# A second mixer's output projection with tokens on partitions, and its norm by token tile

## The chip, the cores and the metric

The kernel runs on one core of one Trainium2 chip. The core has TensorE (PE in the profile), VectorE (DVE), ScalarE (ACT), GpSimd (POOL) and SyncE (SP), a memory of 128 partitions (SBUF) and eight accumulator banks (PSUM), each 512 float32 columns wide, called `pb[0]` to `pb[7]` here. The metric is the device time of the whole program in microseconds, lower is better.

## What is computed

Two blocks in a row on 512 tokens of width 1024, all in float32. The first is an attention block with a feed-forward part, the second is this, and the change lies at its middle:

```python
def second_block(x, ...):
    hn = rms_norm(x, norm_mix_pre)
    mix = hybrid_mixer(hn, ...)               # y = [y_a, y_b]; returns y @ w_out
    x = x + rms_norm(mix, norm_mix_post)
    hn = rms_norm(x, norm_ffn_pre)
    ff = conv_ffn(hn, w_gate, w_up, conv_w, conv_b, w_down)
    return x + rms_norm(ff, norm_ffn_post)

def rms_norm(x, g):
    return x * lax.rsqrt(jnp.mean(x * x, axis=-1, keepdims=True) + EPS) * g

# in hybrid_mixer: four mLSTM heads and four gated linear attention heads of width 128
y_a = sigmoid(a_o) * head_rms_norm(h_fw + h_bw, mlstm_norm)
y_b = silu(b_r) * head_rms_norm(o_fw + o_bw, gla_norm)
y = concatenate([y_a, y_b])                   # 512 tokens x 1024
return y @ w_out
```

`conv_ffn` multiplies hn with two matrices of 1024x2816, runs a convolution over three tokens on one product, and feeds the gated product to `w_down`.

## The kernel before

**Numbers.** Every float32 matmul is three: each operand is split into a high part (rounded for PE's fast float format) and a low part, and `mm3` (L464) adds high*high, low*high and high*low. `AH`/`AL` are the parts of the feed-forward's input, `YH`/`YL` those of the mixer's output, `WH`/`WL` those of the weights.

**Weights.** All weights come as units of 128x1024 float32 (512 KB). There are six slots (`NS`). SP loads unit u into slot u modulo 6 of `RAW` as soon as unit u-6 has been used (`s_used`). GpSimd splits each: a copy into `WH` (L419), a subtraction into `WL` (L422); PE waits for it in `ready`. GpSimd's order is written out by hand, with a few waits by which it is held back; here it gates four heads (L450), makes four low parts of the linear attention heads (L454), waits until all four mLSTM heads are gated (`s_ym`), and splits the rest without further holds.

**Layout.** The residual `X` has features on partitions: 8 tiles (`DK`) of 128 features x 512 tokens. A norm needs a sum over partitions, which PE makes. For the usual norms the sum is wanted late: ACT squares the tiles (L1208), DVE adds them up into `ACC` (L1759, L1762), PE multiplies `ACC` with a constant matrix (`statistic`, L527), ACT takes the root and DVE the reciprocal (`RS`, L1779), which scales the products after the matmul.

**The place of the change.** It begins when the last mLSTM head is done. DVE finishes the heads: the sum of the two directions (L2323), the squares per head (L2242, L2243), the opening by the output gate (L2333), the reciprocal of all sixteen columns (L2390), the gating of each (L2267). PE turns each head (`turn_output`, L1115), ACT makes its high part (L1644) and DVE its low part (L2349). Under this PE starts the output projection with the four linear attention heads: four units side by side in `pb[0]` to `pb[3]`, feature tile m of the result against all 512 tokens; the other four follow one by one. ACT takes each finished bank twice, squared (L1208) and scaled into `MIX` (L1721), and DVE adds up the squares. Then comes the norm "post": PE sums with one-column matmuls (`root_columns`, L542), ACT and DVE make four diagonal matrices of the reciprocal roots, PE broadcasts them (`root_broadcast`, L553), and for each of the eight tiles DVE scales `MIX` (L2403) and adds it to `X` (L2404). ACT makes `AH` (L1206), DVE `AL` (L1752) and the next norm's sum of squares.

**The feed-forward behind it** has 22 chunks (`FC`) of two units (gate and up), which use the banks in three pairs. Its first two chunks, four units, run side by side (L499 to L502), feature tile by feature tile as `AH` and `AL` become ready, with the norm's `statistic` in front of the last tile. In the first block's feed-forward the first two chunks run one after the other, and the statistic stands between the two units of the second.

Of the kernel before, what the change touches and what calls it, by code (L numbers as in the profile page):

```python
# [97 lines left out]
WB = 4  # L98
# [6 lines left out]
def build(nc, dram, out):  # L105

    ctx = ExitStack()
    with ctx:
# [105 lines left out]
        MIX = put("MIX", [P, DK, T], F32, S_at + 32 * KB)  # L214
# [75 lines left out]
        ALL = ("mix", "ffn", "ple", "mix2", "post", "ffn2")  # L290
        SPLIT = tuple(n for n in ALL if n != "post")

        LAST = ("post",)

        def stages(w, names, per, fewer=()):

            s, counts = sem(f"s_{w}"), [per - (n in fewer) for n in names]
            return {n: Stage(s, sum(counts[:i])) for i, n in enumerate(names)}

        s_x = stages("x", ("ffn", "ple", "mix2", "ffn2"), DK)  # L300
        s_gh, s_gl = stages("gh", SPLIT, DK), stages("gl", SPLIT, DK)
# [38 lines left out]
        def state(h, m):  # L340
# [22 lines left out]
        s_vb, s_aof, s_dd, s_ee, s_lv, s_gs, s_gb, s_sad, s_sao, s_go, s_oc, s_ybq = (  # L363
            sem(f"s_{w}") for w in ("vb", "aof", "dd", "ee", "lv", "gs", "gb", "sad", "sao", "go", "oc", "ybq"))
        s_apad, s_a1, s_a3, s_aqk, s_br, s_va, s_zero = (
            sem(f"s_{w}") for w in ("apad", "a1", "a3", "aqk", "br", "va", "zero"))
        s_bc, s_ms2, s_ad, s_w, s_sw, s_mo, s_hb, s_hf, s_hst, s_gn, s_y2t, s_y2h, s_y2l = (
# [43 lines left out]
        def _(pool):  # L411
# [51 lines left out]
        def _(pe):  # L463
# [70 lines left out]

            def root_columns(n):

                ge(pe, s_acc[n], DK - 1)
                for part, src in enumerate((ACC, SQ[:, 1, :])):
                    if part:
                        ge(pe, s_sq[n], DK)  # L540
                    for t in range(NT):
                        ins = nc.tensor.matmul(pb[6][:, t:t + 1], src[:, tokens(t)], INVD[:, 0:1],  # L542
                                               start=(part == 0 and t == 0), stop=(part == 1 and t == NT - 1),
                                               skip_group_check=True)
                ins.then_inc(s_ms[n].sem, 1)

            def root_broadcast(n):
                for t in range(NT):
                    if t < 2:
                        ge(pe, s_diag[n], t + 1)  # L550
                    else:
                        ge(pe, s_adiag[n], t - 1)
                    ins = nc.tensor.matmul(RSP[:, tokens(t)], INVD, DIAG[:, t, :], start=True, stop=True)  # L553
                ins.then_inc(s_bcast[n].sem, 1)
# [303 lines left out]
            for m in range(DK):  # L858
# [9 lines left out]
                if m == 3:  # L868
                    statistic("ple")
# [1701 lines left out]
```

## Time and profile before

| | us |
|---|---|
| median of 3 runs | 1296.03 |
| lowest and highest | 1295.74, 1297.51 |
| the profiled execution | 1295.97 |
| its span | 1294.1 |
| PE busy | 1275.6 (99%) |
| DVE busy | 683.8 (53%) |
| GpSimd busy | 756.2 (58%) |
| ACT busy | 394.2 (30%) |

All times below are microseconds from the start of the profiled execution's span. A row of the chain or of a timeline gives the start, then the length. PE's matmuls are pipelined: the next starts before the last has left the array, so the pace is read from start to start, not from the length. PEclk is the granted clock of TensorE, 1.00 for 2.4 GHz and 0.50 for 1.2 GHz. An instruction that waits is not shown as busy; what released it stands in brackets.

### The profile page before, as it was taken

How to read it: one execution, taken by the hardware profiler on the slowest of the kernel's cores; microseconds unless marked ns; L12 is line 12 of the kernel's file. 1: busy time of each engine (PE TensorE's matmuls, PEld its weight loads, DVE VectorE, ACT ScalarE, POOL GpSimd, SP SyncE). 2: the span in 40 equal slices, each digit the busy share in tenths (PEclk: the TensorE clock that was granted, in tenths of full speed). 3: DMA queues.
4: the chain of work that ended last, by engine and by line, in shares of the span. 5: the costliest groups of instructions: out<-in, count | busy, mean ns of one | idle time of the engine just before them, and what ended most of it. 6: DMA issues, size and time to landing. Idle time of an engine off the chain costs nothing.

```text
span 1294.1 us, 16113 instructions
## 1 busy us (share of the span) xinstructions
PE 1275.6 (99%) x6432; PEld 1042.4 (81%) x6432; DVE 683.8 (53%) x923; ACT 394.2 (30%) x716; POOL 756.2 (58%) x448
## 2 busy tenths in 40 slices
PE   8999999999999999999999999999899999999998
PEld 6888877788888888888888888778788888888886
DVE  5453563887444432123467878684678644447003
ACT  4332474322111111003346365573332211110002
POOL 6855533676666646668665445224649766666660
PEclk9999999999999999999999999999899999999999
DMA  7222211323233323334333122102133223323331
GB/s 287 82 70 78 82 50 50 114 83 97 98 98 98 98 79 107 93 97 132 96 100 99 50 82 82 34 18 82 49 130 94 95 94 96 98 95 98 98 98 65
DMA packets 34207, 117.85 MB, mean 91 GB/s; under 512 B 3812, under 2 KB 4324, under 8 KB 34004
## 3 DMA queue, kind: packets, MB, share of 16 engines
q1 hardware_dynamic: 32976, 114.66, 28.1%
q10 hardware_dynamic: 1156, 2.16, 0.5%
q8 instruction: 51, 0.84, 0.3%
q14 instruction: 24, 0.20, 0.1%
HBM read 114.71 MB, written 2.10 MB: 90 GB/s over the span
## 4 chain that ended last, share of the span: by engine, by line
PE 95%; DVE 3%; ACT 1%; DMA 1%; issue 1%; POOL 0%; SPq 0%; DVEq 0%; ACTq 0%
PE PS L465 28%; PE PS L467 28%; PE PS L466 28%; PE PS L1082 1%; PE PS L967 1%; DVE ACC L1762 1%; PE PS L691 1%; PE PS L668 1%; PE PS L499 1%; PE PS L558 1%; PE PS L500 1%; PE PS L502 1%; PE PS L679 1%; PE PS L950 1%; DMA RAW<-in_w 1%
## 5 line engine op out<-in xcount | busy, mean ns | idle before, releaser
L422 POOL TENSOR_TENSOR WL<-RAW,WH 128x1024 fp32r<-128x1024 f32 (+1 forms) x216 | 509.3, 2358 | 18.0
L419 POOL TENSOR_SCALAR WH<-RAW 128x1024 fp32r<-128x1024 f32 (+1 forms) x216 | 234.4, 1085 | 446.5 <-DMA RAW<-in_w 402.3
L465 PE MATMUL PS<-AH,WH 128*128 128x512 f32 x896 | 351.2, 392 | 2.3 <-POOL WL L422 1.3
L467 PE MATMUL PS<-AH,WL 128*128 128x512 f32 x896 | 348.9, 389 | 0.0
L466 PE MATMUL PS<-AL,WH 128*128 128x512 f32 x896 | 348.7, 389 | 0.0
L465 PEld LDWEIGHTS PS<-AH,WH 128*128 128x128 f32 x896 | 168.2, 188 | 40.6 <-POOL WL L422 2.1
L467 PEld LDWEIGHTS PS<-AH,WL 128*128 128x128 f32 x896 | 168.2, 188 | 35.2
L466 PEld LDWEIGHTS PS<-AL,WH 128*128 128x128 f32 x896 | 168.2, 188 | 34.7 <-issue 0.2
L1407 ACT ACTIVATE TMP<-PAD,PRM 128x512 f32<-128x512 f32 x44 | 35.9, 817 | 125.9 <-DVE PAD L2015 125.9
L1412 ACT ACTIVATE SH<-TMP 128x512 fp32r<-128x512 f32 x44 | 27.8, 632 | 136.9 <-DVE TMP L2030 136.9
L465 PE MATMUL PS<-SH,WH 128*128 128x512 f32 x176 | 68.5, 389 | 0.0
L466 PE MATMUL PS<-SL,WH 128*128 128x512 f32 x176 | 68.5, 389 | 0.0
L467 PE MATMUL PS<-SH,WL 128*128 128x512 f32 x176 | 68.5, 389 | 0.0
L465 PE MATMUL PS<-WH,SH 128*128 128x512 f32 x176 | 68.5, 389 | 0.0
L466 PE MATMUL PS<-WL,SH 128*128 128x512 f32 x176 | 68.5, 389 | 0.0
L467 PE MATMUL PS<-WH,SL 128*128 128x512 f32 x176 | 68.5, 389 | 0.0
L2030 DVE TENSOR_TENSOR TMP<-TMP 128x512 f32<-128x512 f32 x44 | 62.7, 1426 | 7.3 <-ACT TMP L1410 2.8
L2010 DVE TENSOR_TENSOR TMP<-PS,RS 128x512 f32<-128x512 f32 x44 | 30.2, 687 | 67.9 <-PE PS L467 67.9
L2021 DVE SCALAR_TENSOR_TENSOR TMP<-PAD,PRM,TMP 128x512 f32<-128x512 f32 x44 | 44.7, 1015 | 36.6 <-ACT TMP L1407 36.6
L2015 DVE TENSOR_TENSOR PAD<-PS,RS 128x512 f32<-128x512 f32 x44 | 30.3, 688 | 53.1 <-PE PS L467 53.0
L1410 ACT ACTIVATE TMP<-TMP 128x512 f32<-128x512 f32 x44 | 27.8, 633 | 90.3 <-DVE TMP L2024 90.3
L1762 DVE TENSOR_TENSOR ACC<-ACC,SQ 128x512 f32<-128x512 f32 x41 | 47.2, 1150 | 14.0 <-ACT SQ L1208 12.4
(365 smaller groups left out, 2033.0 us busy)
## 6 DMA issues: line engine op xcount, KB each, us to landing
RAW<-in_w SPq DMA_DIRECT2D x185, 512.0 KB, 3.5
RAW<-in_w SPq DMA_DIRECT2D x16, 384.0 KB, 3.0
RAW<-in_w SPq DMA_DIRECT2D x16, 320.0 KB, 2.9
X<-in_x SPq DMA_DIRECT2D x4, 512.0 KB, 6.9
BT<-in_bias SPq DMA_DIRECT2D x1, 2048.0 KB, 9.4
out<-FX SPq DMA_DIRECT2D x4, 256.0 KB, 2.1
out<-FX ACTq DMA_DIRECT2D x4, 256.0 KB, 2.0
PIN<-in_p ACTq DMA_DIRECT2D x1, 512.0 KB, 3.4
```

The source lines that it names most:

```text
L419: nc.gpsimd.tensor_scalar(WH[:, slot, 0:width], RAW[:, slot, 0:width], 1.0, 1.0, ALU.mult, ALU.mult).then_inc(s_hi, 1)
L422: nc.gpsimd.tensor_tensor(WL[:, slot, 0:width], RAW[:, slot, 0:width], WH[:, slot, 0:width].bitcast(F32), ALU.subtract).then_inc(s_split, 1)
L465: nc.tensor.matmul(o, lh, rh, start=start, stop=False)
L466: nc.tensor.matmul(o, lh, rl, start=False, stop=False)
L467: return nc.tensor.matmul(o, ll, rh, start=False, stop=stop)
L1407: A(TMP[:, j, :], PAD[:, j, 0:T], ACT.Identity, bias=prm_at("fcb" + sfx, 0, i, 2, j), scale=prm_at("fcw" + sfx, 0, i, 2, j)).then_inc(S["t ...
L1410: A(TMP[:, j, :], TMP[:, j, :], func).then_inc(S["act"].sem, 1)
L1762: V_.tensor_tensor(ACC[:], ACC[:], SQ[:, j % 2, :], ALU.add).then_inc(s_acc[n].sem, 1)
L2010: V_.tensor_tensor(TMP[:, 2 + j, :], pb[2 * ((2 * i + j) % FB) + 1], RS[:], ALU.mult).then_inc(S["up"].sem, 1)
L2015: V_.tensor_tensor(PAD[:, j, o:o + T], pb[2 * ((2 * i + j) % FB)], RS[:], ALU.mult).then_inc(S["pad"].sem, 1)
L2021: V_.scalar_tensor_tensor(t, PAD[:, j, 1:T + 1], prm_at("fcw" + sfx, FC, i, 2, j), t, ALU.mult, ALU.add).then_inc(S["ta"].sem, 1)
L2030: V_.tensor_tensor(TMP[:, 2 + j, :], TMP[:, j, :], TMP[:, 2 + j, :], ALU.mult).then_inc(S["h"].sem, 1)
```

## The change

It has seven parts.

1. The output projection has tokens on partitions. A unit of weights is now 128 rows of `w_out` in the order `MIXED`, one for each head, and a bank holds 128 tokens x 512 features: banks 2t and 2t+1 are token tile t. `mixed_block` adds one head's product to one bank. PE does six heads for tiles 0 and 1 first, while the heads are turned, then the rest, so that the tiles end one after the other.
2. The norm "post" is made by token tile. ACT squares both banks of a tile with a running sum, takes the root, DVE the reciprocal, ACT writes the scaled product to `MIX`, PE turns it back with eight transposes into the same two banks (`turn_mixed`), and DVE adds it to `X` with the gain (`mixed_added`). The column sums, diagonal matrices and the broadcast are gone.
3. `AH` and `AL` are made in two token sets, tokens 0 to 255 and 256 to 511, eight tiles each.
4. The first chunk of the second feed-forward runs first for one set, then for the other (matmuls of 256 columns); the second chunk runs as a chunk of its own, with the statistic between its two units. The squares for it are made and added after the last `AL`.
5. GpSimd no longer waits for the gated mLSTM heads; it now waits for the last `AL` before it splits the feed-forward's unit 4.
6. The first mLSTM head's root, reciprocal and gating come ahead of the others' squares; the opening and gating of the others are interleaved.
7. The statistic of the first feed-forward stands one unit later, the one of the norm behind it two products later.

The diff, cut to its core:

```diff
-            pool.wait_ge(s_ym, H2)
-            split_range(UNITS["wo2"][0] + 4, UNITS["ffn2"][0] + NS)
-
-            split_range(UNITS["ffn2"][0] + NS, NU)
+            split_range(UNITS["wo2"][0] + 4, UNITS["ffn2"][0] + 4)
+            ge(pool, s_gl["ffn2"], 2 * DK)
+            split_range(UNITS["ffn2"][0] + 4, NU)
...
-                        if root is not None and w == 0:
+                        if root is not None and w == (norm == "ffn"):
                             statistic(root)
...
-                    pe.wait_ge(s_mix, DK)
-                    side_by_side(u0, range(4), AH, AL, (s_gh[norm], s_gl[norm]), {DK - 1: lambda: statistic(norm)})
+                    for u in (u0, u0 + 1):
+                        ready(u)
+                    for part, c in enumerate((FIRST, REST)):
+                        for k in range(DK):
+                            if part == 0 and k == 6:
+                                turn_mixed(NT - 1)
+                            ge(pe, s_gl[norm], DK * part + k + 1)
+                            for w in range(2):
+                                s = (u0 + w) % NS
+                                ins = mm3(pb[w][:, c], WH[:, s, tokens(k)], WL[:, s, tokens(k)], AH[:, k, c],
+                                          AL[:, k, c], k == 0, k == DK - 1)
+                                if part and k == DK - 1:
+                                    ins.then_inc(s_used, 1)
+                    chunk(1, None, norm)
...
-                if m == 3:
+                if m == 5:
                     statistic("ple")
...
                     pe.wait_ge(s_ym, n - H2 + 1)
+                    pe.wait_ge(s_hf, H2)
...
+            def mixed_block(n, t, half, stop=False):
+                k, s, c = MIXED[n], (uw + n) % NS, slice(half * T, (half + 1) * T)
+                return mm3(pb[2 * t + half], YH[:, k, tokens(t)], YL[:, k, tokens(t)], WH[:, s, c], WL[:, s, c],
+                           n == 0, stop)
+
+            def turn_mixed(t):
+                pe.wait_ge(s_pmx, t + 1)
+                for half in range(2):
+                    for q in range(4):
+                        ins = nc.tensor.transpose(pb[2 * t + half][:, tokens(q)], MIX[:, t, tokens(4 * half + q)], IDENT)
+                    ins.then_inc(s_ptt, 1)
+
+            for n in range(6):
+                if n >= 3:
+                    turn_output(H2 + n - 3)
+                ready(uw + n)
+                if n < H2:
+                    pe.wait_ge(s_y2p, n + 1)
                 else:
-                    pe.wait_ge(s_y2l, k + 1)
+                    pe.wait_ge(s_y2l, n - H2 + 1)
+                for t in range(2):
+                    for half in range(2):
+                        mixed_block(n, t, half)
+            turn_output(2 * H2 - 1)
...
+            mixed_pair(6, 2)
+            turn_mixed(0)
+            mixed_pair(7, 2).then_inc(s_mix, 1)
+            turn_mixed(1)
+            mixed_pair(4, 3).then_inc(s_used, 1)
+            mixed_pair(5, 3).then_inc(s_used, 1)
+            turn_mixed(2)
+            mixed_pair(6, 3).then_inc(s_used, 1)
+            mixed_pair(7, 3).then_inc(s_used, 1)
...
+            def mixed_root(t):
+                if t < NT - 1:
+                    act.wait_ge(s_mix, t + 1)
+                else:
+                    act.wait_ge(s_used, UNITS["wo2"][0] + DK)
+                link(A(SQ[:], PS[:, 2 * t:2 * t + 2, :], ACT.Square, accum_out=PSS[:, t:t + 1]))
+                A(PRT[:, t:t + 1], PSS[:, t:t + 1], ACT.Sqrt, bias=EPS_C, scale=1.0 / D).then_inc(s_prt, 1)
...
             for m in range(DK):
-                act.wait_ge(s_used, UNITS["wo2"][0] + m + 1)
-                norm_tile("post", None, m // 2, 2, m % 2, None, x=pb[m % WB], split=False)
-                A(MIX[:, m, :], pb[m % WB], ACT.Copy, scale=prm("post2", m)).then_inc(s_mix, 1)
-            root_of_columns("post")
-            x_tiles("ffn2", "fpre2", AH)
+                if m >= 2:
+                    ge(act, s_acc["ffn2"], m - 1)
+                A(SQ[:, m % 2, :], X[:, m, :], ACT.Square).then_inc(s_sq["ffn2"].sem, 1)
...
+            inverse_roots(0)
+            gated(0)
+            state_squares(1)
             state_sum(H2 - 1)
             state_squares(H2 - 1)
...
+            state_squares(H2 - 2)
+            state_opened(1)
+            inverse_roots(1)
+            gated(1)
+            state_opened(H2 - 2)
+            gated(2)
+            low_turned(range(0, 1))
+            state_opened(H2 - 1)
+            gated(3)
+            low_turned(range(1, H2))
...
+            for k in range(DK):
+                token_low(0, k)
+            mixed_added(2, 0)
+            mixed_reciprocal(3)
+            mixed_added(2, 1)
+            mixed_added(3, 0)
+            mixed_added(3, 1)
+            for k in range(DK):
+                token_low(1, k)
             for m in range(DK):
...
+                add_square("ffn2", m // 2, 2, m % 2)
```

The order on the engines shows it best at three places. The first is GpSimd's queue from the low parts of the linear attention heads on (`YL<-BR,YH`), before:

```order
L454 TENSOR_TENSOR YL<-BR,YH 128x512 [waits s_y2h] x3
L419 TENSOR_SCALAR WH<-RAW 128x1024 [waits s_raw3,s_used,s_ym]
L422 TENSOR_TENSOR WL<-RAW,WH 128x1024 [waits s_hi]
L419 TENSOR_SCALAR WH<-RAW 128x1024 [waits s_raw4,s_used]
L422 TENSOR_TENSOR WL<-RAW,WH 128x1024 [waits s_hi]
```

and with the change:

```order
L452 TENSOR_TENSOR YL<-BR,YH 128x512 [waits s_y2h] x3
L417 TENSOR_SCALAR WH<-RAW 128x1024 [waits s_raw3,s_used]
L420 TENSOR_TENSOR WL<-RAW,WH 128x1024 [waits s_hi]
L417 TENSOR_SCALAR WH<-RAW 128x1024 [waits s_raw4,s_used]
L420 TENSOR_TENSOR WL<-RAW,WH 128x1024 [waits s_hi]
...
L417 TENSOR_SCALAR WH<-RAW 128x1024 [waits s_raw4,s_used]
L420 TENSOR_TENSOR WL<-RAW,WH 128x1024 [waits s_hi]
L417 TENSOR_SCALAR WH<-RAW 128x1024 [waits s_raw5,s_used,s_gl]
L420 TENSOR_TENSOR WL<-RAW,WH 128x1024 [waits s_hi]
```

The wait `s_ym` (the gated heads) has gone from the split behind the `YL` row, and a wait `s_gl` (all `AL`) stands at the split of the ninth unit behind it, unit 4 of the feed-forward.

The second is DVE behind the projection: what scales and adds the product (`MIX`, `X`), makes `AL` and adds the squares (`ACC<-ACC,SQ`). Before, a tile of 512 tokens at a time:

```order
L2403 TENSOR_TENSOR MIX<-MIX,PS 128x512 [waits s_mix,s_bcast]
L2404 TENSOR_TENSOR X<-X,MIX 128x512 [waits s_vc]
L2403 TENSOR_TENSOR MIX<-MIX,PS 128x512 [waits s_mix]
L2404 TENSOR_TENSOR X<-X,MIX 128x512 [waits s_vc]
L1752 SCALAR_TENSOR_TENSOR AL<-X,PRM,AH 128x512 [waits s_gh]
L1759 COPY ACC<-SQ 128x512 [waits s_sq]
L2403 TENSOR_TENSOR MIX<-MIX,PS 128x512 [waits s_mix]
L2404 TENSOR_TENSOR X<-X,MIX 128x512 [waits s_vc]
L1752 SCALAR_TENSOR_TENSOR AL<-X,PRM,AH 128x512 [waits s_gh]
L1762 TENSOR_TENSOR ACC<-ACC,SQ 128x512 [waits s_acc,s_sq]
```

With the change, adds of 128x128 (`X<-PS,PRM,X`), then the two sets:

```order
L2455 SCALAR_TENSOR_TENSOR X<-PS,PRM,X 128x128 [waits s_ptt] x4
L2462 SCALAR_TENSOR_TENSOR AL<-X,PRM,AH 128x256 [waits s_gh] x8
L2455 SCALAR_TENSOR_TENSOR X<-PS,PRM,X 128x128 [waits s_ptt] x4
L2448 RECIPROCAL COL<-COL 128x1 [waits s_prt]
L2455 SCALAR_TENSOR_TENSOR X<-PS,PRM,X 128x128 [waits s_ptt] x12
L2462 SCALAR_TENSOR_TENSOR AL<-X,PRM,AH 128x256 [waits s_gh] x8
L1802 COPY ACC<-SQ 128x512 [waits s_sq]
L1805 TENSOR_TENSOR ACC<-ACC,SQ 128x512 [waits s_acc,s_sq] x7
L1814 RECIPROCAL RS<-RS 128x512 [waits s_sd]
```

The adds into `ACC`, which stood between the `AL`, now stand behind the sixteenth.

The third is PE around the statistic of the second feed-forward (`PS<-ACC,CST`). Before, in front of the last tile of the four units that run side by side:

```order
L502 MATMUL PS<-AL,WH 128x512 [waits s_gl]
L502 MATMUL PS<-AL,WH 128x512 x3
L527 MATMUL PS<-ACC,CST 128x512 [waits s_acc]
L499 MATMUL PS<-AH,WH 128x512 [waits s_gh]
L500 MATMUL PS<-AH,WL 128x512
...
L502 MATMUL PS<-AL,WH 128x512 [waits s_gl]
L502 MATMUL PS<-AL,WH 128x512 x3
L465 MATMUL PS<-AH,WH 128x512 [waits s_split]
```

With the change, from the last tile of the second set on; the cut leaves out the rest of one unit's 24 matmuls:

```order
L462 MATMUL PS<-AH,WH 128x256 [waits s_gl]
L463 MATMUL PS<-AL,WH 128x256
L464 MATMUL PS<-AH,WL 128x256
...
L462 MATMUL PS<-AH,WH 128x512 [waits s_split]
L463 MATMUL PS<-AL,WH 128x512
L464 MATMUL PS<-AH,WL 128x512
...
L464 MATMUL PS<-AH,WL 128x512
L524 MATMUL PS<-ACC,CST 128x512 [waits s_acc]
L462 MATMUL PS<-AH,WH 128x512 [waits s_split]
```

It stands 24 matmuls behind the last one that waits for an `AL`.

## Rows read from the trace of the kernel before

**Rows 1.** The page, part 1 and one group of part 5: busy us, mean ns, idle before
```profile
PE 1275.6 (99%) x6432; PEld 1042.4 (81%) x6432; DVE 683.8 (53%) x923; ACT 394.2 (30%) x716; POOL 756.2 (58%) x448
...
L465 PEld LDWEIGHTS PS<-AH,WH 128*128 128x128 f32 x896 | 168.2, 188 | 40.6 <-POOL WL L422 2.1
```

**Rows 2.** Windows: stretch, its length, busy us (instructions) by engine, PEclk, DMA share, GB/s
```profile
921.00:921.60 0.60, 0.60 (x4) 0.60 (x5) 0.11 (x1) 0.00 (x0) 0.60 (x1) 0.77 0.00 0
...
925.80:931.70 5.90, 5.90 (x14) 4.64 (x15) 5.87 (x8) 2.84 (x5) 1.29 (x1) 0.51 0.01 3
```

**Rows 3.** The chain that ended last: start us, us, what
```profile
889.93 0.44 PE PS L1115 x4
...
917.60 1.75 PE PS L542 x16
...
920.98 1.80 PE PS L553 x8
...
925.77 0.77 PE PS L499
...
936.00 0.91 PE PS L502 x4
...
947.79 0.86 PE PS L527 x2
```

**Rows 4.** Timeline of PE: start us, us, line, operation, [idle before, releaser]
```profile
871.23 0.48 PE L465 MATMUL PS<-YH,WH 128*128 128x512 f32 x1
...
880.09 0.66 PE L1115 MATMUL PS<-CST,YM 128*128 128x128 f32 x4 [0.42 <-DVE YM L2267]
...
195.22 0.28 PE L668 MATMUL PS<-KL,QH 64*128 64x256 f32 x2
195.33 0.28 PE L668 MATMUL PS<-KH,QL 64*128 64x256 f32 x2
```

**Rows 5.** Timeline of DVE, end of the mixer and the norm behind it
```profile
873.98 0.20 DVE L2317 RECIPROCAL COL<-COL 128x8 f32<-128x8 f32 x1
...
875.97 1.12 DVE L2323 SCALAR_TENSOR_TENSOR YM<-PS,COL,TMP 128x128 f32<-128x128 f32 x4
...
879.34 1.29 DVE L2267 SCALAR_TENSOR_TENSOR YM<-YM,COL 128x512 f32<-128x512 f32 x2
...
924.79 0.67 DVE L2403 TENSOR_TENSOR MIX<-MIX,PS 128x512 f32<-128x512 f32 x1
925.50 2.14 DVE L2404 TENSOR_TENSOR X<-X,MIX 128x512 f32<-128x512 f32 x1
927.57 0.74 DVE L1752 SCALAR_TENSOR_TENSOR AL<-X,PRM,AH 128x512 fp32r<-128x512 f32 x1
...
930.54 0.68 DVE L1762 TENSOR_TENSOR ACC<-ACC,SQ 128x512 f32<-128x512 f32 x1
```

**Rows 6.** Timeline of GpSimd, the same stretch
```profile
867.64 5.11 POOL L454 TENSOR_TENSOR YL<-BR,YH 128x512 fp32r<-128x512 f32 x4 [15.49 <-DVE WT L2281]
886.16 1.04 POOL L419 TENSOR_SCALAR WH<-RAW 128x1024 fp32r<-128x1024 f32 x1 [13.41 <-DVE YM L2267]
...
897.47 1.05 POOL L419 TENSOR_SCALAR WH<-RAW 128x1024 fp32r<-128x1024 f32 x1 [4.28 <-DMA RAW<-in_w]
...
924.41 2.68 POOL L422 TENSOR_TENSOR WL<-RAW,WH 128x1024 fp32r<-128x1024 f32 x1
```

**Rows 7.** Timeline of ACT: square and scaled copy of one 512-column bank
```profile
893.83 0.60 ACT L1208 ACTIVATE SQ<-PS 128x512 f32<-128x512 f32 x1 [2.73 <-PE PS L467]
894.32 0.68 ACT L1721 ACTIVATE MIX<-PS,PRM 128x512 f32<-128x512 f32 x1
```

**Rows 8.** Timelines of DVE, GpSimd and PE in the first feed-forward block
```profile
241.93 14.12 DVE L1762 TENSOR_TENSOR ACC<-ACC,SQ 128x512 f32<-128x512 f32 x7
...
241.57 1.16 POOL L419 TENSOR_SCALAR WH<-RAW 128x1024 fp32r<-128x1024 f32 x1 [7.02 <-DVE AL L1752]
...
256.10 1.13 PE L527 MATMUL PS<-ACC,CST 128*128 128x512 f32 x2 [0.57 <-DVE ACC L1762]
```

More of the change, by code:

```diff
@@ L213, in build @@
         WT = put("WT", [P, 3, 2, T], F32, R + 32 * KB)
[L214 removed]
+        MIX = put("MIX", [P, NT, D], F32, S_at + 32 * KB)
         FX = put("FX", [P, NT, D], F32, A_at)
@@ L532, in statistic @@
                 ins.then_inc(s_ms[n].sem, 1)
[L535 to L554, printed above, removed]
             def column_sums(o, src, weights, width):
@@ new lines, in _, with mixed_pair @@
+            turn_output(2 * H2 - 1)
+            def mixed_pair(n, t):
+                for half in range(2):
+                    ins = mixed_block(n, t, half, n == DK - 1)
+                return ins
+            pe.wait_ge(s_y2l, 2)
+            mixed_pair(0, 2)
+            mixed_pair(1, 2)
+            pe.wait_ge(s_y2l, H2)
+            mixed_pair(0, 3).then_inc(s_used, 1)
+            mixed_pair(1, 3).then_inc(s_used, 1)
+            for n in (2, 3):
+                mixed_pair(n, 2)
+                mixed_pair(n, 3).then_inc(s_used, 1)
@@ new lines, in _ @@
+            for n in (4, 5):
+                mixed_pair(n, 2)
+            for n in (6, 7):
+                ready(uw + n)
+                for t in range(2):
+                    ins = mixed_pair(n, t)
+                    if n == 7:
+                        ins.then_inc(s_mix, 1)
+            mixed_pair(6, 2)
[4 more added lines that the diff above has]
+            mixed_pair(5, 3).then_inc(s_used, 1)
@@ L1386, in _ @@
                 mixed_high(j)
-            def x_tiles(n, gain, hi):
-                for m in range(DK):
-                    norm_tile(n, gain, m // 2, 2, m % 2, hi)
             for m in range(DK):
@@ L1664, in scaled_states, with mixed_roots @@
                 ins.then_inc(s_hst, 1)
+            def mixed_roots(part):
+                act.wait_ge(s_mq, part + 1)
+                m = MSS[:, ROOTS[part]]
+                A(m, m, ACT.Sqrt, bias=EPS_C, scale=1.0 / DV).then_inc(s_gn, 1)
             stabilisers_copied(0)
@@ L2389, in _ @@
-            dve.wait_ge(s_gn, 2)
-            link(V_.reciprocal(MSS, MSS))
-            gated(0)
-            for h in range(H2):
-                if h + 1 < H2:
-                    gated(h + 1)
-                low_turned(range(h, h + 1))
-            for m in range(DK - 1):
-                add_square("post", m // 2, 2, m % 2)
-            column_reciprocal("post")
-            ge(dve, s_bcast["post"], 1)
-            for m in range(DK):
-                dve.wait_ge(s_mix, m + 1)
-                link(V_.tensor_tensor(MIX[:, m, :], MIX[:, m, :], RSP, ALU.mult))
-                V_.tensor_tensor(X[:, m, :], X[:, m, :], MIX[:, m, :], ALU.add).then_inc(s_x["ffn2"].sem, 1)
-                if m:
-                    low("ffn2", "fpre2", (m - 1) // 2, 2, (m - 1) % 2, AH, AL)
-                    add_square("ffn2", (m - 1) // 2, 2, (m - 1) % 2)
@@ new lines, in mixed_added, with token_low @@
+            def mixed_added(t, half):
+                for q in range(4):
+                    k = 4 * half + q
+                    dve.wait_ge(s_ptt, 2 * t + half + 1)
+                    x = X[:, k, tokens(t)]
+                    ins = V_.scalar_tensor_tensor(x, pb[2 * t + half][:, tokens(q)], prm("post2", k), x, ALU.mult, ALU.add)
+                    if t % 2:
+                        ins.then_inc(s_x["ffn2"].sem, 1)
+            def token_low(part, k):
+                c = REST if part else FIRST
+                ge(dve, s_gh["ffn2"], DK * part + k + 1)
+                V_.scalar_tensor_tensor(AL[:, k, c], X[:, k, c], prm("fpre2", k), AH[:, k, c].bitcast(F32),
+                                        ALU.mult, ALU.subtract).then_inc(s_gl["ffn2"].sem, 1)
@@ new lines, in _ @@
+            mixed_reciprocal(0)
+            for t in range(2):
+                mixed_added(t, 0)
+                mixed_reciprocal(t + 1)
+                mixed_added(t, 1)
+            for k in range(DK):
+                token_low(0, k)
[4 more added lines that the diff above has]
+            mixed_added(3, 1)
+            for k in range(DK):
+                token_low(1, k)
+            for m in range(DK):
+                add_square("ffn2", m // 2, 2, m % 2)
```

106 lines of the change are left out of this document (47 added, 59 removed).

## The prediction

> **What bounds the kernel now.** The first view is the page: PE is busy for 99% of the span [rows 1], so time is lost only where PE stops, does extra work, or runs on a slower clock. The second is the chain that ended last, read from the second mixer's output projection to the first two chunks of the second feed-forward block. It runs through matmuls except at one place [rows 3]. PE starts the projection at 871.23 [rows 4]; the last column sums of its norm start at 917.60 and take 1.75; a wait of 1.6 follows, the broadcast takes 1.80 from 920.98, and the next matmul starts at 925.77, 3.0 later. The third is the windows view: the granted clock is at 0.77 in 921.0 to 921.6, so it fell from 2.4 to 1.2 GHz there, after sixteen one-column matmuls and the wait of 1.6, and it is still at 0.51 in 925.8 to 931.7 [rows 2]. 5.7 us of resumed matmuls at half speed lose 2.85. The statistic of the next norm ends at 948.65, and twelve more matmuls of 0.2275 (four take 0.91 [rows 3]) end the two chunks at 951.4. That is my milestone; behind it PE has nothing to wait for up to the end of the span, with or without the change.
>
> Over the pure work the stretch holds: a wait of 0.5 at the first turned head [rows 4], 1.75, 1.6, 1.8, 3.0 and 2.85, together **11.5 us**. That is the most this change can win here.
>
> **What the matmuls cost after it.** The projection keeps 192 matmuls of 512 columns. Of the first two chunks, one keeps 48, the other becomes 96 of 256 columns. No row shows a full-height 256-column one. The nearest is a pair of 64-row ones, 0.11 apart [rows 4], which would be half of 0.2275; the other end is the mean duration of a weight load, 0.188 [rows 1]. I take 0.115, since weight loads of the four turned tiles follow each other at 0.11 (0.44 for four [rows 3]), though each lasts longer: +0.1 for 96. The upper end costs 96 times 0.073, 7.0. The Trainium skill (TensorE: Matmul & The Clock Gate, LDWEIGHTS) puts a weight load of 128 columns at 107 ns; no row here shows that duration, and an estimate from that page would make the sum 0.6 less.
>
> **The norm's new form.** 32 transposes at 0.11 are **+3.5**. They replace 1.75 and 1.8 of PE work and the waits of 1.6 and 3.0. A token tile's chain is a square of 1024 columns, a root, a reciprocal and a scaled copy. From 0.60 and 0.68 for 512 columns [rows 7] I take 1.03 and 1.2 (bounds: no growth, and double), with 0.45 for the two small steps: 2.7. Behind the first tile PE has 12 matmuls, 2.73, so it waits 0.15 to 0.25. At the second tile the reciprocal stands on DVE behind four adds (1.12 for four from PSUM [rows 5]), and PE has only the first turn and 6 matmuls: 0.75. The third tile has 12 matmuls over it: nothing. Together **+1.0**. These adds have one input in PSUM, and such an operation kept 0.67 while GpSimd worked [rows 5, 6].
>
> **The second token set.** PE ends the first set and turns the fourth tile inside it. DVE must then do eight adds (2.25) before the first AL of the rest. PE comes there at 871.23 + 43.7 (192 matmuls) + 1.76 (turned heads) + 3.65 (waits at them, below) + 1.0 + 2.64 (24 transposes) = 924.0 for the first set, whose 48 matmuls and 8 transposes last 5.5 + 0.9: 930.4. The fourth tile is turned after 36 of these, from 928.1 to 929.0; DVE's adds behind the halves end at 930.9 and the first AL at 931.3: **+0.95**. From there PE needs 48 times 0.115, 5.5, while DVE makes the other seven AL in some 2.5 (half of 0.74 [rows 5] and a start each). So the last AL is done 2.5 after the first, and PE arrives behind the first unit of the next chunk at 5.5 plus 24 times 0.2275, **8.45 us after the last AL**.
>
> **The statistic.** PE needs all eight squares added up there, and DVE adds none before the last AL. Before, these adds lay between the AL, and GpSimd had nothing to split from 927.1 on, since its slots were full. Now the last AL is just what GpSimd waits for. The first feed-forward block already has this arrangement: GpSimd starts its splits at 241.57, with the last AL, and seven adds take 14.12, to 256.05 [rows 8]; one alone takes 0.68 [rows 5]. So the adds end 14.5 after the last AL and **PE waits 14.5 - 8.45 = 6.1**. Even in the first block, where more matmuls lie over them, PE waited 0.57 [rows 8]. The queue behind the waiting statistic holds the next 24 matmuls, and nothing can overtake it. The raw halves of units 4 and 5 are long in their slots then (a load lands some 3.6 after its slot is free [rows 6]), so GpSimd does have work. A wait of 6.1 is longer than the 3.7 from the last wide matmul to 921.3, when the clock fell [rows 2, 3]; I take the same loss as before, **+2.85** (bounds 0 and 2.85).
>
> **The heads.** GpSimd's wait for the gated heads goes. Its YL end at 872.75 and its next split stood until 886.16 [rows 6]; now two splits fill 872.8 to about 880.9. DVE's chain there has two inputs in SBUF at each square, gating and opening. The price of the overlap is read off one such operation: X<-X,MIX took 2.14, where an add alone takes 0.68 [rows 5], while GpSimd's subtraction ran from 924.41 [rows 5, 6]; it ended only behind it. Laid out so, with reciprocal done at 874.1 [rows 5]: the first head is gated at 877.2 instead of 875, sum of the fourth head (which the turn now also waits for) at 880.4, second gating at 884.8, first YL at 886.75. PE arrives at 879.4, 883.6 and 885.3, so it waits 1.0, 1.25 and 1.4: **+3.65**. With no overlap it would wait only 0.9, at the first YL, as that now stands behind two gatings. The Trainium skill (SBUF — State Buffer, Who interferes with whom) says that a DVE operation with both inputs in SBUF takes an exclusive lock against GpSimd's reads, for whole instructions. No row shows this for the gating itself; by that rule the head waits stand at 3.65 and not at 0.9.
>
> **Splits.** Units 6 and 7 of the projection are loaded when the third and fourth token tiles release units 0 and 1, at 897.4 and 898.8, are split by 904.5 and 908.0, and PE needs them at 906.75 and 909.5: cover 1.5 at the least.
>
> **Elsewhere.** The first block's statistic one unit later takes away its 0.57: **-0.6**. The third statistic, two products later, had no wait and has none; what it feeds is needed far later, I take 0 (bounds 0 and 1).
>
> **The sum.** After: 3.5 + 1.0 + 0.95 + 6.1 + 2.85 + 3.65 + 0.1 = 18.15. Less 11.5 and 0.6: **+6.05**. The profiled execution took 1295.97, within 0.1 of the median 1296.03, so 1302.0.
>
> **Rivals.** (1) Faster: the adds do not meet the splits as they did in the first block. The point is 1.15 us an add: below it, seven adds and a copy are done within 8.45 and PE never waits. Alone they cost 0.68, 4.8 in all. Then 6.1 and 2.85 go: 1293.1, and 1290.3 if the heads escape the overlap too. Against it stands that forms, sizes and the starting event are those of the first block. (2) The wait comes, the clock holds: 1299.2. For it: PE did no narrow matmuls ahead. (3) 256-column matmuls cost a weight load each: 7.0 more, of which the slower second set takes 3.5 off the statistic's wait: 1305.5. Against it, the transposes' 0.11. (4) Overlaps are half of what I take, and gain and loss cancel: 1296.
>
> **Chances.** Forecast 0.50 (own range 1299.5 to 1304.5), (1) 0.20, (2) 0.13, (3) 0.10, (4) 0.07. The range 1292.5 to 1305.5 leaves out the better half of (1) and the tail of (3). A measurement of this kernel tells some 0.2%, 2.6 us, from no change. Faster 0.20, within it 0.16 (case 4, part of 2, the edge of the forecast), slower 0.64.
>
> **What would show it.** Right: PE idle some 6 us before the second block's statistic, released by ACC; seven adds in some 14 us beside splits; a granted clock near 0.5 right behind; three waits of over a microsecond at the turned heads. Each is wrong alone if its row reads otherwise. The whole is wrong if the adds run at under 1.15 each; the chain would then go through matmuls from 872 on, and all that is left of the 11.5 are transposes and waits of 9.2.

## The result and the profile after

The changed kernel takes **1302.95 us** (median of 6 runs, 1300.27 to 1304.77) where the kernel before takes 1296.77 (6 runs, 1295.29 to 1298.17): a ratio of 1.0052, interval 1.0041 to 1.0064. It is slower, by 6.2 or 0.5%. Its profiled execution took 1300.27, the fastest of the six, with a span of 1298.4.

The timeline of PE at the turned heads, the turned token tiles, the second token set and the statistic (columns as in [rows 4]; before, the first of these places had one wait of 0.42, and [rows 3] shows the others):

```profile
878.42 0.63 PE L1104 MATMUL PS<-CST,YM 128*128 128x128 f32 x4 [0.74 <-issue]
...
882.90 0.66 PE L1104 MATMUL PS<-CST,YM 128*128 128x128 f32 x4 [1.10 <-DVE YM L2302]
...
884.99 0.47 PE L462 MATMUL PS<-WH,YH 128*128 128x512 f32 x1 [1.43 <-DVE YL L2386]
...
912.22 1.09 PE L1137 MATMUL PS<-CST,MIX 128*128 128x128 f32 x8 [0.16 <-ACT MIX L1746]
...
930.16 0.39 PE L462 MATMUL PS<-AH,WH 128*128 128x256 f32 x1 [0.78 <-DVE AL L2462]
...
941.25 0.39 PE L464 MATMUL PS<-AH,WL 128*128 128x512 f32 x1
947.41 2.07 PE L524 MATMUL PS<-ACC,CST 128*128 128x512 f32 x2 [5.77 <-DVE ACC L1805]
948.50 1.42 PE L462 MATMUL PS<-AH,WH 128*128 128x512 f32 x1
```

The first stop stands as "issue", that is, its row names no releaser. By the code the turn also waits for the fourth head's sum (`s_hf`), and DVE's row of it ends at 878.32, 0.10 ahead of PE:

```profile
877.20 1.12 DVE L2358 SCALAR_TENSOR_TENSOR YM<-PS,COL,TMP 128x128 f32<-128x128 f32 x4
```

The long wait is the predicted one, and its releaser is the add into `ACC`. DVE and GpSimd in the same stretch show why (the answering rows of before are [rows 5, 6], and the pattern is that of [rows 8]):

```profile
932.80 0.42 DVE L1802 COPY ACC<-SQ 128x512 f32<-128x512 f32 x1
933.32 14.04 DVE L1805 TENSOR_TENSOR ACC<-ACC,SQ 128x512 f32<-128x512 f32 x7
```

```profile
932.97 1.17 POOL L417 TENSOR_SCALAR WH<-RAW 128x1024 fp32r<-128x1024 f32 x1 [4.36 <-DVE AL L2462]
934.22 2.71 POOL L420 TENSOR_TENSOR WL<-RAW,WH 128x1024 fp32r<-128x1024 f32 x1
936.90 1.49 POOL L417 TENSOR_SCALAR WH<-RAW 128x1024 fp32r<-128x1024 f32 x1
```

GpSimd's splits start with the last `AL`, and the chain of waits shows the adds in step with them: they last about 1.36 and 2.71 in turn, and each of the seven ends 0.54 to 0.56 behind the end of a GpSimd instruction (934.68 behind 934.14, 937.48 behind 936.93).

```profile
933.32 1.36 DVE ACC L1805
934.77 2.71 DVE ACC L1805
937.58 1.35 DVE ACC L1805
939.03 2.71 DVE ACC L1805
```

The windows view (columns as in [rows 2]) shows the clock: the fall of before at 921 is gone, and it is at 0.50 around the resumed matmuls instead.

```profile
921.00:921.60 0.60, 0.60 (x4) 0.50 (x3) 0.60 (x3) 0.56 (x2) 0.27 (x1) 1.00 0.57 157
943.50:944.50 1.00, 0.00 (x0) 0.00 (x0) 1.00 (x1) 0.33 (x1) 1.00 (x1) 0.86 0.84 344
944.50:950.00 5.50, 2.59 (x4) 1.46 (x5) 2.75 (x2) 0.47 (x1) 5.42 (x4) 0.50 0.04 11
...
950.60:951.20 0.60, 0.60 (x3) 0.50 (x2) 0.60 (x1) 0.00 (x0) 0.54 (x1) 0.63 0.00 0
951.20:956.00 4.80, 4.80 (x22) 3.95 (x22) 4.44 (x4) 1.62 (x2) 1.86 (x1) 1.00 0.00 0
```

The ledger against the trace. The stretch from the projection's first matmul to the end of the first two chunks was 80.02 (871.23 to 951.25) and is 86.30 (869.26 to 955.56). Each term is read from start to start here, since the idle time in brackets counts from the modelled end of the last matmul and leaves out 0.16 to 0.26 of each stop (941.25 + 0.23 to 947.41 is 5.93, the bracket says 5.77).

| term, us | predicted | measured |
|---|---|---|
| 32 transposes | 3.5 | 3.5 (eight take 0.79, and the next wide matmul 0.09 more) |
| waits at the turned token tiles | 1.0 | 1.1 |
| second token set | 0.95 | 0.95 |
| the second statistic | 6.1 | 5.95 |
| half clock behind it | 2.85 | 1.8 |
| turned heads | 3.65 | 3.85 (0.90, 1.26, 1.69) |
| 96 matmuls of 256 columns | 0.1 | 0.6 (0.12 apart) |
| what was there before | -11.5 | -11.5 (taken over, not read anew) |
| sum | +6.65 | +6.25, the stretch grew by 6.28 |
| ahead of the projection | -0.6 | -1.97 |
| profiled execution, milestone | +6.05 | +4.31 |

### The profile page after: what moved, and what is told of

Its sections match the earlier page's. It is cut to its first block, busy times and chain, and to the rows that moved or that the text cites. A ratio compares the mean times of both kernels' runs of the same rounds, so it can differ in the third digit from the quotient of the medians.

```text
span 1298.4 us, 16239 instructions
## 1 busy us (share of the span) xinstructions
PE 1275.3 (98%) x6488; PEld 1043.1 (80%) x6488; DVE 677.9 (52%) x942; ACT 395.0 (30%) x722; POOL 751.6 (58%) x448
## 4 chain that ended last, share of the span: by engine, by line
PE 94%; DVE 3%; ACT 1%; DMA 1%; issue 0%; POOL 0%; SPq 0%; DVEq 0%; ACTq 0%
PE PS L462 29%; PE PS L464 28%; PE PS L463 28%; PE PS L1070 1%; PE PS L955 1%; DVE ACC L1805 1%; PE PS L667 1%; PE PS L644 1%; PE PS L534 1%; PE PS L655 1%; PE PS L938 1%; DMA RAW<-in_w 1%; PE PS L1051 0%; PE PS L929 0%; PE PS L540 0%
## 5 line engine op out<-in xcount | busy, mean ns | idle before, releaser
L417 POOL TENSOR_SCALAR WH<-RAW 128x1024 fp32r<-128x1024 f32 (+1 forms) x216 | 231.3, 1071 | 455.7 <-DMA RAW<-in_w 420.9
L462 PE MATMUL PS<-AH,WH 128*128 128x512 f32 (+1 forms) x944 | 367.9, 390 | 3.5 <-DVE AL L1795 1.5
L464 PE MATMUL PS<-AH,WL 128*128 128x512 f32 (+1 forms) x944 | 364.3, 386 | 0.0
L463 PE MATMUL PS<-AL,WH 128*128 128x512 f32 (+1 forms) x944 | 364.3, 386 | 0.0
L462 PEld LDWEIGHTS PS<-AH,WH 128*128 128x128 f32 x944 | 177.6, 188 | 43.3 <-issue 3.0
L464 PEld LDWEIGHTS PS<-AH,WL 128*128 128x128 f32 x944 | 177.5, 188 | 36.2
L463 PEld LDWEIGHTS PS<-AL,WH 128*128 128x128 f32 x944 | 177.6, 188 | 35.8 <-issue 0.8
L2065 DVE TENSOR_TENSOR TMP<-TMP 128x512 f32<-128x512 f32 x44 | 55.0, 1251 | 7.0 <-ACT TMP L1423 2.8
L2068 DVE TENSOR_TENSOR SL<-TMP,SH 128x512 fp32r<-128x512 f32 x44 | 36.5, 829 | 30.7 <-ACT SH L1425 30.7
```

The lines of the kernel that those rows point to most:

```text
L417: nc.gpsimd.tensor_scalar(WH[:, slot, 0:width], RAW[:, slot, 0:width], 1.0, 1.0, ALU.mult, ALU.mult).then_inc(s_hi, 1)
L462: nc.tensor.matmul(o, lh, rh, start=start, stop=False)
L463: nc.tensor.matmul(o, lh, rl, start=False, stop=False)
L464: return nc.tensor.matmul(o, ll, rh, start=False, stop=stop)
L2065: V_.tensor_tensor(TMP[:, 2 + j, :], TMP[:, j, :], TMP[:, 2 + j, :], ALU.mult).then_inc(S["h"].sem, 1)
L2068: V_.tensor_tensor(at(SL, i, j, 2), TMP[:, 2 + j, :], at(SH, i, j, 2).bitcast(F32), ALU.subtract).then_inc(S["sl"].sem, 1)
```

## The experiments

Kernels of before beside the three groups of runs took 1296.21 (21 runs), 1295.83 (28) and 1295.87 (26). Each experiment starts from the changed kernel unless it says otherwise.

**1. GpSimd held until the adds are done.**

```
-            ge(pool, s_gl["ffn2"], 2 * DK)
+            ge(pool, s_acc["ffn2"], DK)
```

> The changed kernel, but GpSimd stays held until DVE has added the last square of the second feed-forward's norm, and not only until the last AL. Theory (the seven adds meet GpSimd's splits): the adds take some 4.8 us instead of 14.0, PE does not wait at the statistic, the granted clock stays at 1.00; the wait of 5.8 and 1.75 of half clock go, 1303.0 becomes about 1295.5, ratio to the kernel before 0.999. Rival (the adds are slow by themselves, or ACT's squares set their pace): they stay at 14, the statistic waits as before, 1303. Second rival (GpSimd starts 5 us later and PE waits for unit 4 instead): the wait moves to the start of the third chunk, and less than half is won.

Measured: 1294.94 (11 runs), ratio 0.9993 (0.9984 to 1.0002). DVE's timeline:

```profile
933.76 5.47 DVE L1805 TENSOR_TENSOR ACC<-ACC,SQ 128x512 f32<-128x512 f32 x7
```

PE does not wait at the statistic. The mean clock of the profiled execution is 1.0, that of the ten others 0.996 to 0.998. One line of waiting moved on GpSimd is worth 8.0 in the medians (7.6 by the ratios); the 5.95 and the 1.8 of clock behind it make 7.75. The splits start 6.4 later (939.32 for 932.97) and cost nothing: PE waits for none.

**2. The statistic 24 matmuls later.**

```
-                        if root is not None and w == (norm == "ffn"):
+                        if root is not None and w == 1:
```

> The changed kernel, but the second feed-forward's statistic stands one unit (24 matmuls, 5.45 us) later; the splits still run beside the adds. Theory (only the place of the statistic against the end of the adds matters): the adds still take 14.0, PE waits 0.3 to 0.6 at the statistic, the clock stays at 1.00, about 1296.0, ratio 0.999. Rival (the slow adds or the late reciprocal root cost PE elsewhere, at the banks): less than 4 us is won.

Measured: 1295.99 (11 runs), ratio 0.9994 (0.9985 to 1.0002). The adds are as slow as ever, and PE is there only 0.4 too early (timelines of DVE and of PE):

```profile
935.64 14.11 DVE L1805 TENSOR_TENSOR ACC<-ACC,SQ 128x512 f32<-128x512 f32 x7
```

```profile
949.80 1.13 PE L524 MATMUL PS<-ACC,CST 128*128 128x512 f32 x2 [0.40 <-DVE ACC L1805]
```

So the cost sits in where PE asks for the sum, not in DVE's time. This is the other cure for the same collision.

**3. Work in place of the wait.** If the clock falls because PE stands idle, it should hold when PE works through that time. The 24 extra matmuls go to the free bank `pb[7]`, and nothing reads them.

```
+                            if norm == "ffn2":
+                                ready(u + 1)
+                                for k in range(DK):
+                                    mm3(pb[7], WH[:, (u + 1) % NS, tokens(k)], WL[:, (u + 1) % NS, tokens(k)],
+                                        AH[:, k, :], AL[:, k, :], k == 0, k == DK - 1)
```

> The changed kernel with 24 more matmuls of 512 columns into an unused bank in front of the second feed-forward's statistic; their result is not used. They last 5.45 us and lie in the wait of 5.8. Theory (the idle time costs twice: the wait, and the half clock behind it): the wait shrinks to some 0.3, the adds end when they did, the clock stays at 1.00, and 1.75 us are won for added work: 1301.2, ratio 1.0035. Rival (the clock's loss is not due to the idle time): no gain, 1303.

Measured: 1301.64 (5 runs), ratio 1.0041 (1.0029 to 1.0054). A window that holds the end of the adds, in this kernel:

```profile
943.50:950.00 6.50, 6.10 (x25) 4.40 (x24) 4.35 (x4) 1.32 (x2) 6.42 (x3) 1.00 0.18 71
```

The clock stays at 1.00. From the statistic to the sixth matmul behind it PE now takes 2.12 (947.95 to 950.07), in the changed kernel 3.84 (947.41 to 951.25): 1.7 less, the clock's own share, which agrees with the 1.8 of the ledger and is below my 2.85. The median falls by 1.3, but the intervals of the two ratios overlap, so the time alone does not show it; the traces do.

**4. Why the adds are slow: their squares in PSUM.** GpSimd's hold is that of the change; only ACT writes the squares to two free banks.

```
-                A(SQ[:, m % 2, :], X[:, m, :], ACT.Square).then_inc(s_sq["ffn2"].sem, 1)
+                A(pb[6 + m % 2], X[:, m, :], ACT.Square).then_inc(s_sq["ffn2"].sem, 1)
...
+                sq = pb[6 + j % 2] if n == "ffn2" else SQ[:, j % 2, :]
...
-                    V_.tensor_tensor(ACC[:], ACC[:], SQ[:, j % 2, :], ALU.add).then_inc(s_acc[n].sem, 1)
+                    V_.tensor_tensor(ACC[:], ACC[:], sq, ALU.add).then_inc(s_acc[n].sem, 1)
```

> The changed kernel, with only the place of the second norm's squares changed: ACT writes them into the two banks pb[6] and pb[7], which are free then, instead of SBUF, and DVE adds them up from there. GpSimd is held back no longer than in the changed kernel, so its splits still run beside all seven adds. Theory: an add is stretched by a split because both its inputs lie in SBUF; with one in PSUM it takes its 0.7, the seven take 5 us beside splits, and the statistic's wait and the half clock go: 1294.9, as with GpSimd held (1294.94). Rival: the splits stretch whatever DVE does there, by the traffic as such; then the adds stay at 14 and the time at 1302.5. In between (adds of 1.15 to 1.5) the wait would be 0 to 3.

Measured: 1294.91 (11 runs), ratio 0.9992 (0.9984 to 1.0001). DVE and GpSimd side by side:

```profile
937.00 5.44 DVE L1806 TENSOR_TENSOR ACC<-ACC,PS 128x512 f32<-128x512 f32 x7
```

```profile
936.39 1.05 POOL L417 TENSOR_SCALAR WH<-RAW 128x1024 fp32r<-128x1024 f32 x1 [4.37 <-DVE AL L2463]
937.52 2.41 POOL L420 TENSOR_TENSOR WL<-RAW,WH 128x1024 fp32r<-128x1024 f32 x1
939.91 1.04 POOL L417 TENSOR_SCALAR WH<-RAW 128x1024 fp32r<-128x1024 f32 x1
```

The same seven adds beside the same splits take 5.44 instead of 14.04, and the splits take 1.05 and 2.41 instead of 1.49 and 2.71. The operation, its size and its neighbour are unchanged; what changed is the place of the second input, and with it where ACT writes. ACT's writes are not the cause: in experiment 1 they go to SBUF as before and the adds take 5.47. So for these adds the condition is that both inputs lie in SBUF while GpSimd splits. The Trainium skill (SBUF — State Buffer, Who interferes with whom) says that a DVE instruction with two SBUF inputs contends with a GpSimd instruction that reads SBUF, and one with at most one such input does not. The traces agree, with 14.04 against 5.44.

**5. The first head's low part first.** DVE makes it right behind the second gating, ahead of the other openings.

```
             gated(1)
+            low_turned(range(0, 1))
             state_opened(H2 - 2)
             gated(2)
-            low_turned(range(0, 1))
```

> The changed kernel, but DVE makes the first mLSTM head's low part right behind the second head's gating and not behind the third's. Theory (the low part stands behind an opening and a gating that nobody waits for): PE's wait of 1.4 at the fifth head's product falls to some 0.2 and nothing else moves, -1.2 us, 1301.8, ratio 1.004. Rival (the next turned head or the fourth gating becomes late): less than 0.5 won, with a new wait at a later turned head.

Measured: 1301.33 (5 runs), ratio 1.0041 (1.0028 to 1.0053). The wait of 1.43 is gone, but the one at the second turned head is 2.14 in this execution:

```profile
884.56 0.89 PE L1104 MATMUL PS<-CST,YM 128*128 128x128 f32 x4 [2.14 <-DVE YM L2302]
```

On its own it is not told from no effect (the ratios' intervals overlap). Together with experiment 1 it is:

> The changed kernel with two edits that were also run alone: GpSimd held until the squares of the second norm are added up (alone: 1294.9), and the first head's low part ahead of the openings of the others (alone: 1301.3 against 1302 to 1303). The second one only moved a wait in its own run (2.14 at the second turned head in the place of 1.10 and 1.43). If the head waits are worth nothing to order within DVE's chain, the time is that of the first edit: 1294.9; if each microsecond of the low part's wait counts, it is 1293.8.

Measured: **1292.81** (10 runs), ratio 0.9972 (0.9963 to 0.9981), below experiment 1 by more than the intervals, and below both of my numbers. I had taken its wait as merely moved. From start to start the head stops are 0.87, 1.28 and 1.68 in experiment 1, 3.8 together, and one of 2.30 here: 1.5 less. Experiment 4's execution, in which DVE's rows at the heads last as long as here, has stops of 2.30 and 1.68: 1.7 less. The medians differ by 1.6 (changed kernel) and 2.1 (experiment 1). This is the lowest median of all kernels here, 3 below the kernel before; two that follow (1293.0 and 1293.16) are not told from it.

**6. No splits beside the heads.** GpSimd splits the projection's units 4 and 5 ahead of its work for the linear attention heads.

```
-            split_range(UNITS["ffn"][0] + 3, UNITS["wo2"][0] + 4)
+            split_range(UNITS["ffn"][0] + 3, UNITS["wo2"][0] + 5)
...
+            split_range(UNITS["wo2"][0] + 5, UNITS["wo2"][0] + 6)
...
-            split_range(UNITS["wo2"][0] + 4, UNITS["ffn2"][0] + 4)
+            split_range(UNITS["wo2"][0] + 6, UNITS["ffn2"][0] + 4)
```

> The changed kernel, but GpSimd splits the projection's units 4 and 5 ahead of its work for the linear attention heads (one before the products into YB, one before the YL), so that it has no split left beside DVE's chain of the mLSTM heads. Theory, from the profile of the changed kernel: the gating there takes 2.77 and 1.52 where it would take 1.4 and 1.3 alone, because each ends only with a split; the three head waits (0.74, 1.10 and 1.43, together 3.27) shrink to 1.0 or less, and the time is 2.3 below the changed kernel's: 1300.5 with 1296.2 for the kernel before. Rival: the chain of operations, not the overlap, sets these waits; then they stay within 0.5 of 3.27 and the time stays at 1302.5. The statistic's wait grows by nothing in either case: 5.8 stays.

Measured: 1302.45 (6 runs), ratio 1.0054 (1.0035 to 1.0074). The time is the rival's, the mechanism is not. PE has no wait at the heads, and DVE's gating and square take 0.69 and 0.68:

```profile
878.05 0.69 DVE L2303 SCALAR_TENSOR_TENSOR YM<-YM,COL 128x512 f32<-128x512 f32 x1
878.66 0.68 DVE L2278 TENSOR_TENSOR TMP<-YM 128x512 f32<-128x512 f32 x1
```

In the changed kernel these two stood beside splits:

```profile
872.34 2.77 DVE L2302 SCALAR_TENSOR_TENSOR YM<-YM,COL 128x512 f32<-128x512 f32 x1
875.03 1.52 DVE L2277 TENSOR_TENSOR TMP<-YM 128x512 f32<-128x512 f32 x1
```

But both splits now fall beside DVE's work inside the mLSTM loop. Unit 5's raw half lands only at 858.3; beside its split four operations take 3.90 that took 1.14, and PE waits:

```profile
858.58 3.90 DVE L2359 SCALAR_TENSOR_TENSOR YM<-NUM,COL,TMP 128x128 f32<-128x128 f32 x4 [0.20 <-ACT TMP L1677]
```

```profile
863.39 2.45 PE L1071 MATMUL PS<-VA,WT 128*128 128x129 f32 x10 [1.09 <-DVE WT L2327]
```

The projection starts at 875.51, 6.25 later than in the changed kernel. Read at the same matmuls of both traces, 2.06 of this are there ahead of both splits (821.32 for 819.26), in code that is the same. Unit 4's split costs 1.08 (835.54 to 841.53 is 5.99, it was 4.91; PE waits 0.61 and 0.23). Unit 5's costs 3.11 (861.34 to 869.73 is 8.39, it was 5.28): the wait, and behind it a clock of 0.54 from 864.0 to 867.5. So the two moved splits cost 4.2 and save 3.85 at the heads, and the time stays. The collision was moved, not removed. In the fastest kernel, that of experiment 5 with both edits, it is the same:

> The changed kernel with three edits: GpSimd held until the squares are added up, the two early splits, and the first head's low part first. If overlap sets both the statistic's wait (5.8) and the head waits (3.3), both go: 1302.5 less 8.0 (statistic and clock, as measured by the first edit alone), less 2.3 for the heads, and up to 0.9 for the low part: 1291.5 to 1292.5, which would be 4 below the kernel before. If the head waits are DVE's chain alone, 1294.9 as with the first edit alone.

Measured: 1293.0 (11 runs), ratio 0.9978 (0.9969 to 0.9986); without the early splits it was 1292.81. Then only one of the two splits was moved, to behind the second gating, on the fastest kernel:

```
+            split_range(UNITS["wo2"][0] + 4, UNITS["wo2"][0] + 5)
+            pool.wait_ge(s_ym, 2)
+            split_range(UNITS["wo2"][0] + 5, UNITS["ffn2"][0] + 4)
```

> The best version so far (GpSimd held until the squares are added up, first head's low part first: 1292.8), and GpSimd's split of the projection's unit 5 held until two mLSTM heads are gated. Theory: a split costs DVE about 1.5 wherever DVE has two inputs in SBUF. The square of the second head that took 2.15 takes 0.68, so the second turned head comes 1.5 earlier and its wait of 2.14 is 0.7; but the split then runs beside the openings and gatings of the other heads, which get 1.5 to 3 longer, and unit 5 is split at 886.5 to 887, where PE needs it at 887.9. Net 0 to -1: 1292.3. If only the wait at the second head counts: 1291.4. If unit 5 comes late: above 1293.5.

Measured: 1294.38 (11 runs), ratio 0.9988 (0.9979 to 0.9997), 1.6 worse in the medians, with intervals that just overlap (0.9963 to 0.9981 there); I had said 1292.3. DVE's timeline shows the collision at its new place:

```profile
883.52 2.77 DVE L2304 SCALAR_TENSOR_TENSOR YM<-YM,COL 128x512 f32<-128x512 f32 x1
```

PE stops three times instead of once, for 0.84, 0.89 and 1.68 from start to start, 3.4 for 2.3. I had priced the overlap and forgotten the third head's turn behind it.

**7. Both cures.** Squares in PSUM with the low part first, without the longer hold:

> The same with the first head's low part first, which together with GpSimd held gave 1292.8. If the place of the squares replaces the hold fully: 1292.8, and 1.3 to 2 lower than with the squares in SBUF by as much as GpSimd's earlier splits could be worth, which I take as 0, since PE waited for no split in any run. If the adds are still stretched: 1301.3, as with the low part alone.

Measured: 1293.16 (10 runs), ratio 0.9976 (0.9967 to 0.9985), the same as with the hold. GpSimd's earlier splits are worth nothing, as PE waits for none.

**8. Part 7 of the change alone, on the kernel before.**

```
-                        if root is not None and w == 0:
+                        if root is not None and w == (norm == "ffn"):
```

> The kernel before with one part of the change alone: the statistic of the first feed-forward block one unit later. By the ledger this takes away a wait of 0.57 and nothing else: 1295.6 with 1296.2 for the kernel before. Rival: a wait downstream swallows it, and the time stays within 0.2. Both are near what can be told apart; the profile is to show whether the wait is gone and whether the milestones behind it (the mixer's last head, the projection's start at 871.2) come 0.6 earlier. If they come 2.0 earlier, as in the changed kernel, this part alone explains all of that; if 0.6, the other 1.4 belong to the parts that touch the mLSTM heads.

Measured: 1294.85 (11 runs), ratio 0.9992 (0.9984 to 1.0001). The wait is gone (timeline of PE):

```profile
260.79 1.02 PE L527 MATMUL PS<-ACC,CST 128*128 128x512 f32 x2
```

From 820.85 to the projection at 870.41 this kernel takes 49.56, the kernel before 49.50 (821.73 to 871.23), the changed one 48.73 (820.53 to 869.26). The projection starts 0.82 earlier than in the kernel before, and 0.27 of that is there at 190 already, where no edit lies. So part 7 gives its 0.6 and not the 0.77 that the changed kernel gains in the mLSTM loop. That gain comes at one place: at 860.6 the kernel before has this row, and the changed one has the same ten matmuls without a wait, in 1.38.

```profile
860.59 1.76 PE L1082 MATMUL PS<-VA,WT 128*128 128x129 f32 x10 [0.25 <-DVE WT L2291]
```

Before, DVE has three operations for a finished head there, from 857.79 to 859.80, ahead of the one that PE waits for; the changed kernel has them elsewhere (part 6). That this is the cause was not tried by itself.

## Why the prediction was right, and where it was off

The direction, the place and the mechanism were right. That the total came within 1 us of the median is partly luck, as the last point shows.

- **What bounds it, and the end of it.** Right. Behind the milestone the traces run alike: 4.31 at the milestone, 4.3 in the spans.
- **The statistic.** Right, in place, releaser and size: 5.95 for 6.1. Adds of 14.04 for 14.1, GpSimd starting with the last `AL`, PE there 8.6 behind it for 8.45. Experiments 1, 2 and 4 each take it away by another link of the chain, with the same 7 to 8 us. Rival (1), adds that escape the splits, is what experiments 1 and 4 produce; its 1293.1 was 1.8 too low.
- **The clock.** The term that was mis-sized most: 1.8 for 2.85. I took the loss of another place over. There the half clock lasted 5.7 of resumed work, here it was over 3.6 behind the restart (947.41 to 951.0). Rival (2), that it holds, was wrong: 0.50 in the window.
- **The heads.** Right, 3.85 for 3.65, and step by step: the chain runs as laid out, shifted by the 2.0 that all of it comes earlier (first head gated at 875.1 for 877.2, second at 882.85 for 884.8, first `YL` at 884.85 for 886.75). The stops are 0.90, 1.26 and 1.69 for 1.0, 1.25 and 1.4. The overlap with the splits, which made the difference between 0.9 and 3.65, is there: gating and square take 2.77 and 1.52 beside splits, 0.69 and 0.68 without. The 0.9 itself was not seen: with no split at the heads (experiment 6) PE does not stop there at all, though DVE's chain also starts 0.5 earlier against the projection in that execution.
- **Turned tiles and second set.** Right. ACT's square of 1024 columns takes 1.03 and the scaled copy 1.12, for 1.03 and 1.2.
- **256-column matmuls.** 0.12 apart for 0.115. Rival (3), a weight load's 0.188 each, is excluded. So is the other side, a pace below 0.115: the sum that the prediction puts 0.6 lower for it (96 times 0.008 would be 0.8) is not borne out.
- **Ahead of the projection.** The gain in the mLSTM loop (0.77) was not priced at all: I looked at where the heads end and not at what else DVE's queue held up. The rest of the 1.97 (0.4 of it is there at 190, where both kernels do the same) belongs to no edit.
- **The median.** The profiled execution gives +4.3, the medians +6.2. I expected the profile to stand at the median. The six executions of the changed kernel go with their mean clock: 1300.3 at 0.996, 1302.8 at 0.995 (three), 1304.6 at 0.994 (two). What can differ is seen at the heads. In the profiled executions of the changed kernel and of experiments 1 and 3, DVE's gating and the next two squares take 2.77, 1.52 and 1.00, and the clock stays at 1.00. In those of experiments 2, 4, 5 and 7 the same code takes about 1.55, 2.88 and 2.15, as in the fastest kernel:

```profile
872.46 1.54 DVE L2302 SCALAR_TENSOR_TENSOR YM<-YM,COL 128x512 f32<-128x512 f32 x1
873.93 2.88 DVE L2277 TENSOR_TENSOR TMP<-YM 128x512 f32<-128x512 f32 x1
```

Already the sum ahead of it, beside GpSimd's last `YL`, takes 3.27 in the first group and 2.14 in the second, so the gating starts 3.1 or 2.0 behind the projection and meets another GpSimd instruction: here the copy (872.42 to 873.47), in the changed kernel the subtraction (872.17 to 874.56). It ends 0.53 or 0.55 behind it. The first stop at the heads then goes, the second grows, and the clock falls behind it, in experiment 2 so:

```profile
880.00:886.00 6.00, 2.36 (x12) 1.56 (x11) 5.86 (x11) 1.57 (x3) 0.00 (x0) 1.00 0.00 0
886.00:890.00 4.00, 4.00 (x12) 3.13 (x11) 1.53 (x3) 0.00 (x0) 0.00 (x0) 0.59 0.00 0
```

That costs some 1.6 of clock (4.0 of matmuls at 0.59 instead of 1.00) and 0.2 more of stops (2.37 and 1.69, 4.06 for 3.85). My forecast of 1302.0 thus came close through two misses that offset each other: a gain upstream not seen (1.4), and a profiled execution 2.7 faster than the median. Which part of the 2.7 is the heads is open: no profile of a median execution was taken. A part can also lie upstream, as the projection starts at 869.26 in the changed kernel's profile and at up to 870.96 (experiment 4) in executions of kernels that are the same up to there.

## What to carry to other kernels

When a reordering makes one engine's release the start of another's work, ask what DVE does at that moment: operations with two SBUF inputs ran at GpSimd's pace here. There are three cures, and each was worth 7 to 8 us here: hold GpSimd until the chain is through, ask for the result later, or put one operand into PSUM. Moving the collision to another place only moved the wait, in all three kernels that tried it (experiment 6), so look for the place where PE has cover, not for a place that is free on GpSimd.

## What the runs showed of the hardware

- An add of 128x512 with one input in PSUM took 0.69 beside GpSimd's splits (seven in 5.44). With both inputs in SBUF it took 1.35 or 2.71, and ended some 0.55 behind the end of a GpSimd instruction; the splits too were slower then (1.49 and 2.71 for 1.05 and 2.41).
- Which GpSimd instruction a DVE operation meets can differ between executions though the code up to there is the same: the gating of the first head took 2.77 in three profiled executions (changed kernel, experiments 1 and 3) and 1.55 in five (experiments 2, 4, 5 twice, 7).
- The time of one and the same kernel goes mostly with its mean granted clock: the kernel with all three edits (experiment 6) took 1295.0 at 0.996 (four executions) and 1291.6 at 0.999 (five).
- At the turned heads the clock stayed at 1.00 behind idle times of 0.7, 1.1 and 1.4 (three executions). It fell behind 2.2 and 1.4 (0.59 in experiment 2), behind 2.1 alone (0.63 in 884 to 888 of the fastest kernel), and behind 0.7, 0.7 and 1.4 (0.56 in 888.3 to 892 of the last kernel of experiment 6).
- A stop of PE costs 0.16 to 0.26 more than the idle time that the timeline prints beside it.
